# The first phase of a fused decoder block cut into five k ranges in place of four

## What is computed

```python
c_act = silu(c)
mod = c_act @ ada_w + ada_b                      # ada_w: 2048 x 12288
sh1, sc1, g1, sh2, sc2, g2 = split(mod, 6)
u = rms_norm(x, mix_norm_pre) * (1 + sc1) + sh1  # 256 x 2048
proj = u @ w_in                                  # w_in: 2048 x 16384
...
x = x + (1 + g1) * rms_norm(merged @ w_out, mix_norm_post)
u = rms_norm(x, ffn_norm_pre) * (1 + sc2) + sh2
x = x + (1 + g2) * rms_norm(conv_ffn(u), ffn_norm_post)
```

## Time and profile before

| | |
|---|---|
| median of 3 runs | 1881.23 us (1879.52 to 1882.01) |
| the profiled execution's own time | 1878.78 us |
| its span from first to last instruction | 1877.0 us |
| mean granted TensorE clock | 0.988 |
| TensorE matmul busy | 1830.4 us (98%), 8980 matmuls |
| VectorE busy | 1322.4 us (70%) |
| ScalarE busy | 870.4 us (46%) |
| transfers | 432.67 MB, mean 231 GB/s |

### The profile page before, as it was taken

The page is one execution under the profiler, slowest core; times in us unless marked ns, Lnnn a source line. Parts: engine busy times, 40 slices in busy tenths (PEclk is TensorE's granted clock), DMA queues, the critical chain, the costliest instruction groups (busy, mean ns, idle before and its releaser), DMA issues.

```text
span 1877.0 us, 25391 instructions
## 1 busy us (share of the span) xinstructions
PE 1830.4 (98%) x8980; PEld 1545.0 (82%) x8980; DVE 1322.4 (70%) x1896; ACT 870.4 (46%) x1005; POOL 100.8 (5%) x141
## 2 busy tenths in 40 slices
PE   5999999999999999999999989999999999999998
PEld 5888888888888888888878868888888888888886
DVE  4888787778676777687887566776777777754455
ACT  4533444344454545463434546444444444444444
POOL 0000011111111111111110000000000000000000
...
GB/s 350 386 351 326 192 247 256 251 258 260 270 241 273 240 269 253 275 235 269 271 271 194 239 157 135 193 188 180 194 185 183 196 181 186 193 188 194 197 184 110
DMA packets 247793, 432.67 MB, mean 231 GB/s; under 512 B 10308, under 2 KB 101108, under 8 KB 247088
## 3 DMA queue, kind: packets, MB, share of 16 engines
...
## 4 chain that ended last, share of the span: by engine, by line
PE 77%; DMA 9%; DVE 9%; issue 3%; ACT 1%; SPq 0%; POOLq 0%; DVEq 0%; ACTq 0%
PE ps L878 18%; PE ps L540 10%; PE ps L542 10%; PE ps L541 10%; PE ps L881 9%; DMA ada_ring<-in_ada_w 8%; PE ps L920 4%; PE ps L918 4%; PE ps L919 4%; DVE w_low L1328 3%; DVE ada_acc L1354 3%; PE ps L656 1%; PE ps L562 1%; PE ps L658 1%; PE ps L657 1%
## 5 line engine op out<-in xcount | busy, mean ns | idle before, releaser
L1328 DVE TENSOR_TENSOR w_low<-stage,w_high 128x1024 fp32r<-128x1024 f32 x608 | 742.5, 1222 | 321.3 <-ACT w_high L964 304.0
L964 ACT ACTIVATE w_high<-stage 128x1024 fp32r<-128x1024 f32 x552 | 584.1, 1061 | 792.7 <-PE ps L542 418.7
L540 PE MATMUL ps<-w_high,lhs 128*128 128x512 f32 x1280 | 507.6, 397 | 0.9 <-DVE w_low L1328 0.8
L542 PE MATMUL ps<-w_high,lhs 128*128 128x512 f32 x1280 | 500.7, 391 | 0.0
L541 PE MATMUL ps<-w_low,lhs 128*128 128x512 f32 x1280 | 500.2, 391 | 0.0
L878 PE MATMUL ps<-lhs,w_high 128*128 128x512 f32 x1408 | 386.2, 396 | 2.2 <-issue 2.2
L1354 DVE SCALAR_TENSOR_TENSOR ada_acc<-ada_ring,c_act,ada_acc 128x256 f32<-128x256 f32 x480 | 230.6, 480 | 120.0 <-DMA ada_ring<-in_ada_w 116.9
L542 PEld LDWEIGHTS ps<-w_high,lhs 128*128 128x128 f32 x1280 | 241.4, 189 | 51.5
L540 PEld LDWEIGHTS ps<-w_high,lhs 128*128 128x128 f32 x1280 | 241.6, 189 | 51.1 <-issue 1.8
L541 PEld LDWEIGHTS ps<-w_low,lhs 128*128 128x128 f32 x1280 | 241.7, 189 | 48.6
L878 PEld LDWEIGHTS ps<-lhs,w_high 128*128 128x128 f32 x1408 | 241.7, 190 | 35.1 <-issue 2.5
...
## 6 DMA issues: line engine op xcount, KB each, us to landing
...
ada_ring<-in_ada_w POOLq DMA_DIRECT2D x128, 512.0 KB, 6.4
...
```

The source lines that it names most:

```text
L540: pe.matmul(acc, hi, w_high[:, slot, k, :], start=kt == 0, stop=False)
L542: last = pe.matmul(acc, lo, w_high[:, slot, k, :], start=False, stop=kt == KT - 1)
L964: act.activation(w_high[:, h % 4, :, :], stage[:, slot, 2 * (h % 2):2 * (h % 2) + 2, :], ACT.Copy).then_inc(high_ready, 1)
L1328: dve.tensor_tensor(w_low[:, h % 4, :, :], stage[:, slot, 2 * (h % 2):2 * (h % 2) + 2, :], w_high[:, h % 4, :, :].bitcast(F32), ALU.subtra ...
```

## The change

k is cut into five ranges of 1, 2, 2, 2 and 1 pairs. A stage of one pair has 4 MiB of modulation, in four slots of four k tiles x 256 columns x 2. Stage 0 has no direct part any more (`ada_steps(0)` is 16, and `direct_slot(0)` lies behind the last slot), so `direct_sums(0, 0, 16)` is gone, and `sum_first(0)` itself begins the accumulation. The direct slot of later stages is the middle one and not the last but one. `sum_first(1)` stands behind RK0 of stage 0, the others behind RQ0. The direct sums are spread over the groups of `DIRECT_IN`. The last stage's order is gb0, RV, gb1, RQ, gb2, RK, gb3. The 56 units remain, each with the same 12 matmuls: stage 0 is units 0 to 6, then come 7 to 20, 21 to 34, 35 to 48 and 49 to 55 (before: 0 to 13, 14 to 27, 28 to 41, 42 to 55).

```diff
--- before.py
+++ after.py
@@ -56,10 +56,11 @@
 RV0, RQ0, RK0 = 4, 5, 6
 FIRST_COLS = (COL_GB, COL_GB + NC, COL_GB + 2 * NC, COL_GB + 3 * NC, COL_RV, COL_RQ, COL_RK)
 FIRST_BANKS = (6, 6, 6, 6, 2, 0, 4)
-FIRST_PAIRS = ((0, 1), (2, 3), (4, 5), (6, 7))
+FIRST_PAIRS = ((0,), (1, 2), (3, 4), (5, 6), (7,))
 STAGES = len(FIRST_PAIRS)
-FIRST_ORDER = ((0, 1, RV0, 2, 3, RQ0, RK0),) * (STAGES - 1) + ((RV0, 0, 1, RQ0, 2, 3, RK0),)
-SUM_BEHIND = (RQ0,) * (STAGES - 1) + (None,)
+FIRST_ORDER = ((0, 1, 2, 3, RV0, RQ0, RK0),) * (STAGES - 1) + ((0, RV0, 1, RQ0, 2, RK0, 3),)
+SUM_BEHIND = (RK0,) + (RQ0,) * (STAGES - 2) + (None,)
+DIRECT_IN = ((RV0, RQ0, RK0),) + ((RV0, RQ0),) * (STAGES - 2) + ((),)
 FIRST_END = {}
 for _st in range(STAGES):
     for _g in FIRST_ORDER[_st]:
@@ -360,11 +361,11 @@
 
         def ada_steps(st):
 
-            return KT - ada_rows(st)
+            return KT - ada_rows(st) if st else KT
 
         def direct_slot(st):
 
-            return ada_slots(st) - 2
+            return ada_slots(st) // 2 if st else ada_slots(st)
 
         def ada_row(st, i):
 
@@ -428,7 +429,7 @@
                 if q >= 4:
                     st_, slot_ = (st, slot - 4) if slot >= 4 else (st - 1, ada_slots(st - 1) + slot - 4)
                     if slot_ == direct_slot(st_):
-                        sp.wait_ge(ada1_direct, st_ + 1)
+                        sp.wait_ge(ada1_direct, st_)
                     else:
                         sp.wait_ge(ada1_step, steps_through(st_, slot_))
                 rows_, width = ada_rows(st), ada_width(st)
@@ -613,7 +614,7 @@
                 width = 4 * len(FIRST_PAIRS[st])
                 for i in range(width):
                     last = pe.matmul(ps[:, 7, i:i + 1], ada_acc1[:, st % 2, i * P:(i + 1) * P], ones[:, 0:1],
-                                     start=False, stop=i == width - 1)
+                                     start=st == 0 and i == 0, stop=i == width - 1)
                 last.then_inc(ada1_summed, 1)
 
 
@@ -635,8 +636,11 @@
                         last = multiply(2 * pair + k, FIRST_BANKS[g], (n + i) % 4, k)
                         if k == 1:
                             last.then_inc(used, 1)
-                        if g == SUM_BEHIND[st] and (i, k) != (0, 0):
-                            direct_sums(st + 1, (None, 0, 4, 10)[2 * i + k], (None, 4, 10, 16)[2 * i + k])
+                        if g in DIRECT_IN[st]:
+                            pieces = 2 * len(FIRST_PAIRS[st]) * len(DIRECT_IN[st]) - 1
+                            m_ = 2 * (len(FIRST_PAIRS[st]) * DIRECT_IN[st].index(g) + i) + k - 1
+                            if m_ >= 0:
+                                direct_sums(st + 1, 16 * m_ // pieces, 16 * (m_ + 1) // pieces)
 
             def first_streamed(n, st, j, summed):
 
@@ -667,10 +671,9 @@
             for n in range(4):
                 last = pe.transpose(ps[:, 5, n * 88:(n + 1) * 88], conv_rows[:, n, :], ident[0:88, 0:88])
             last.then_inc(cols_turned, 1)
-            keep_warm(16)
-            direct_sums(0, 0, 16)
+            keep_warm(8)
             sum_first(0)
-            keep_warm(14)
+            keep_warm(8)
             n = 0
             for st in range(STAGES):
                 summed = st + 1
```

## The result

| | before | after |
|---|---|---|
| median (5 runs each, side by side) | 1881.23 us | 1891.67 us (1887.97 to 1897.57) |
| ratio | | 1.0056, 95% interval 1.0037 to 1.0076 |
| the profiled execution's own time | 1878.78 | 1890.36 |
| its span | 1877.0 | 1888.5 |
| unit 0 begins | 46.84 | 33.26 |

The change costs 0.56%. The forecast was "no change", 1882.7 with a range of 1878.0 to 1888.0, so it was wrong, and the median lies above the range. The start came as worked out, to 0.04 us, which is closer than its terms were. Unit 7 began 2.9 us later than forecast and unit 56 6.8 us later. Of the 11.5 us between the two spans 8.2 are there at unit 56; the other 3.3 arise behind it.

A forecast was written before the change was run, and what follows sets the result against it. TensorE, busy 1830 of 1877 us, was taken as the bound. Unit 56: 66.9 + 156.1 - 1.0 + 1.6 + 0.3 = 223.9 against 222.45, +1.5 us, so 1882.7 us on the median, "no change"; range 1878.0 to 1888.0.

The forecast's parts named there:

- The start: Ahead of unit 0: VectorE's narrow steps end at 28.4 and unit 0 begins at 33.3, 13.5 us earlier.
- Short rows: Stage 0's transfers: 1 KiB rows of `ada_w` cost 1.2 us more for 4 MiB (0 to 1.4).
- Unit 7 at 66.9: End of stage 0: sum_first(1) begins at 61.9, then 1.9 sum and 3.0 lhs chain; before, unit 7 was at 66.35.
- up to 2: VectorE ahead of sum_first(1): up to 2 us more where units 7 to 9 wait for their weights.
- 1.9 for the sum: TensorE at sum_first(1): the sum takes 1.9 us, begun at 61.9 and followed by the lhs chain.
- half clock *around* unit 7: TensorE around sum_first(1): idle, one-column sum, idle bring half clock, costing 1.6 us (0 to 3.8).
- Rival A: Around unit 7: half clock lasts 13.5 us, some 59 matmuls become 38; +6.3 us in all, 1887.5; chance 0.15.
- 0.9 if the clock is full, and nothing if TensorE is slowed: Stage 1 from unit 7: VectorE needs about 37.7 us, TensorE 36.8; 0.9 at full clock, nothing if TensorE is slowed.
- -1.0 for the last sum: Last range's sum ahead of unit 56: 8 rows fewer, 1.0 us less.
- A shift of unit 56 should reach the end whole: Behind unit 56: the rest of the kernel is untouched, so its shift reaches the end whole.
- +0.3 for the rotations: Last stage: two more additions come ahead of the rotations TensorE waits for; +0.3 us (0 to 1.2).
- Rival B: Transfers around unit 7: stage 2's first slot lands late or the rate is 358 GB/s; 1885.6 to 1887.5; chance 0.15.

The follow-up runs named there:

- e1: The changed kernel with 20 warm-up pairs ahead of sum_first(1) and 12 behind it; ratio to the kernel before 1.0024.
- e19: The changed kernel, 12 warm-ups behind sum_first(1), VectorE's later steps of stages 1 and 2 half wide, stage 1's modulation loads halved; ratio to the kernel before 1.0002.
- e8: The changed kernel with the direct slot last but one again; ratio to the kernel before 1.0074.
- e12: The changed kernel, 20 warm-ups ahead of sum_first(1) and 12 behind, VectorE's later steps of stage 1 half wide; ratio to the kernel before 1.0046.
- e20: The changed kernel with the last stage in the order RV, gb0, gb1, RQ, gb2, gb3, RK; ratio to the kernel before 1.0045.
- e21: The changed kernel, last stage ordered RV, gb0, gb1, RQ, gb2, gb3, RK, 20 warm-ups ahead of sum_first(1) and 12 behind; ratio to the kernel before 1.0035.
- e17: The changed kernel with 12 warm-ups behind sum_first(1) and stage 1's modulation loads half as long; ratio to the kernel before 1.0031.
- e13: The changed kernel with 20 warm-ups ahead of sum_first(1) and 12 behind, stage 1's modulation loads half as long; ratio to the kernel before 1.0025.
- e18: The changed kernel, 12 warm-ups behind sum_first(1), stage 1's later VectorE steps half wide and its modulation loads half as long; ratio to the kernel before 1.0019.
- e16: The changed kernel with 12 warm-ups behind sum_first(1) and VectorE's later steps of stage 1 half wide; ratio to the kernel before 1.0034.
- e10: The kernel before with stage 0's direct part given to VectorE, 8 warm-ups ahead of the first sum and 8 behind; ratio to the kernel before 1.0001.
- e11: The kernel before with stage 0's direct part given to VectorE, 60 warm-ups ahead of the first sum and 12 behind; ratio to the kernel before 1.0003.
- e2: The changed kernel with sum_first(1) behind RQ0 and direct sums in RV0 and RQ0 in stage 0 too, unit 6 covering the lhs chain; ratio to the kernel before 1.0033.

## Why the prediction was wrong, by its own steps

**The start: right.** Steps 0.82 apart: measured 0.79 to 0.80, end 28.0 for 28.4. Short rows: from 10 to 30 us the transfers moved 345 and 371 GB/s where they had moved 372 and 387, which is 0.43 MB, 1.1 us at 387 (1.2 taken). The Trainium skill (DMA: Bandwidth & Descriptors, Why small descriptors are slow) led to an estimate of 0.5 by its 3 beats a packet; the trace is nearer twice that. The sum ran at half clock (1.86 for 8 rows, 1.0 forecast), which hid beside the step of stage 1. The chain began at 30.0 (30.3 forecast) and took 3.2 (3.0): that unit 0 came within 0.04 us is partly luck.

**Unit 7 at 66.9: too early by 2.9.** Two terms. The last steps ended at 63.1 and not 61.9, since VectorE was held 2.9 us by data (1.70 and 1.16), more than the "up to 2" allowed; its busy time was about right (26.8 for 26.5). And "1.9 for the sum" was 3.6: I had put the half clock *around* unit 7 at 1.6 in all, but it took that in the sum alone (3.57 against 1.95 in e1) and 1.8 more in unit 7 (4.9 against 3.1). The mechanism (idle, one-column sum, idle) was named and only its size was off. Each stretch was priced too low as well: matmuls start 0.427 us apart at half clock (115.36 to 118.35 in the change) and 0.227 at full, so 3.4 us of it cost 1.6 and not 1.1; "9 matmuls in 3.2 us" counts one that only ends in the window. Rival A, at 0.15, had the length right, 13.7 us at 0.50, and the mechanism only in part: it filled them with 59 matmuls, 4.8 us (6.3 by the distances above), where TensorE stood idle for 5.6 of them and the cost was 3.4, in the sum and unit 7. That its 1887.5 is nearer to the result than the forecast is luck; it was still 4 short, since it left VectorE out.

**"0.9 if the clock is full, and nothing if TensorE is slowed": the step that failed.** VectorE needs 40.8 from unit 7 to the next sum, not 37.7. Its busy time was right (35.4 in e1); its waits were 5.4, not 1.8. Most of them (4.1) are waits for `w_high`, and ScalarE in turn may be only four units ahead of TensorE, for which it waited 23.5 us. TensorE needs 37.5. So the gap is 3.3 us. And the exemption for a slowed TensorE is wrong: with a slow unit 7, VectorE waited 2.04 for bank 6 ahead of its first addition and ScalarE for `used`, so slow clock delays the work that was to catch up, and both terms add: in the table of six runs above narrow steps take 3.3, 3.1 and 2.8 us off, and a slow unit 7 adds 1.1 to 2.3, with full steps and with narrow ones. In e19, where the steps are narrow and the sum no longer waits, unit 7 to 56 takes 156.5.

**-1.0 for the last sum, stages 3 and 4: right.** The sum's rows took 0.9 less, and stage 4 19.04, seven units without a wait. Units 35 to 49 took 42.8 for 46.1 before, 2.3 more than the rows explain; the kernel before has its half-clock stretch of 178.6 there (1.6) and waits of 0.35, the change neither.

**"A shift of unit 56 should reach the end whole": wrong.** I had +0.3 for the rotations (0 to 1.2). The wait grew by 0.45, but a half-clock stretch of 3.4 us follows it at 244.9 in most five-range profiles (not in e1, e8, e12, e20, e21), so with the change's order units 56 to 65 took 28.5 (without the stretch) to 30.1 (with it) against 28.0. The remaining 1.2 of the span lie further on, and the stretch behind unit 65 differs by more between profiles of kernels that are the same there (1626.8 in e17 to 1633.5 in e13).

**Rival B** was right as a mechanism in a kernel that was not this one: it holds unit 7 to about 8 us behind the end of the direct part (e18, e19). In the changed kernel the sum begins 4.5 us behind that end and covers it; in e16, where it begins 1.5 behind, VectorE's step already waits 1.63. Its other half, a rate of 358 GB/s, did not hold: the windows of the change with a full queue and no 1 KiB rows ran at 386 to 388, and the long one from 34 to 60 at 376. The Trainium skill (DMA: Bandwidth & Descriptors, Where 436 GB/s comes from) names that figure as the HBM side's limit; these windows disagree.

The sum of it at unit 56: +3.5 at unit 7, +3.3 for VectorE in stage 1, +1.8 for the slow unit 7, -1.0 for the last sum, which is 7.6 of 8.2. The rest, 0.6, is what is left of larger terms: against the kernel before, units 7 to 21 took 0.9 more than these terms, units 21 to 35 2.1 more, and units 35 to 49 2.3 less. Most of the two last is half clock in other places (3.4 us of it at 163 in the change, at 178.6 before, 1.6 us each); the 0.9 I can't assign. Open is why the half-clock stretches come in some executions and not in others; they make each position above uncertain by one or two times 1.6 us.

No variant beat the kernel before; e10, e11 and, with half of two ranges' sums left out, e19 equal it. Two things were not tried: the first step of stage 2 behind `lhs_pair`, against rival B's wait, and e2's cover with the clock kept up.
